# Expert layers that take four experts at a time in every step, with the first weight places given back in halves, and the decay gates of all heads of the gated linear attention made at once

## The reference

```python
def gla_mixer(x, w_in, gate_w, gate_b, norm_g, w_out):
    z = x @ w_in
    q, k, v, r, glr = jnp.split(z, [...], axis=-1)
    loga = log_sigmoid(einsum('bsgr,grk->bsgk', glr, gate_w) + gate_b) / 16     # decay gates, 4 heads, 2 directions
    o = gla_chunked(q, k, v, loga_forward) + flipped(gla_chunked(... loga_backward))
    return (silu(r) * head_norm(o, norm_g)) @ w_out

def ec_moe(x, w_router, w_gate, w_up, w_down):                                  # 16 experts, 32 tokens each
    aff = softmax(einsum('bnd,de->bne', x, w_router))
    gates, idx = top_k(swapaxes(aff, 1, 2), 32)
    xin = x[bidx, idx]
    h = silu(einsum('becd,edf->becf', xin, w_gate)) * einsum('becd,edf->becf', xin, w_up)
    out = einsum('becf,efd->becd', h, w_down) * gates[..., None]
    return zeros_like(x).at[bidx, idx].add(out)

for i in range(2):
    h = (mlstm_mixer if i == 0 else gla_mixer)(x, ...)
    x = layer_norm(ALPHA * x + h, ...)
    x = layer_norm(ALPHA * x + ec_moe(x, ...), ...)
```

## Time and profile before

| | |
|---|---|
| median of the runs | 2774.12 us (2769.06 to 2780.21) |
| the profiled execution | 2774.46 us, span of its instructions 2772.7 us |
| mean granted TensorE clock | 0.962 |
| busy: PE, DVE, ACT, POOL | 2492.2, 1249.6, 955.9, 77.7 us |
| moved by DMA | 692.63 MB, 250 GB/s over the span |
| matmuls of L1849 | 453.3 us gate and up, 203.9 us down |
| PE idle before L1849, ended by DMA | mostly `weight_ring<-in_moe_w_gate`, 50.4 us |

### The profile page before, as it was taken

One profiled execution on the slowest core, in us unless ns is written; L12 is line 12 of the kernel. 1 busy time (PEld: TensorE's weight loads), 2 busy tenths in 40 slices (PEclk: granted clock), 3 DMA queues, 4 the chain that ended last, 5 costly groups with the idle time before them and its releaser, 6 DMA issues.

```text
span 2772.7 us, 32444 instructions
## 1 busy us (share of the span) xinstructions
PE 2492.2 (90%) x13553; PEld 1716.4 (62%) x13553; DVE 1249.6 (45%) x1906; ACT 955.9 (34%) x1526; POOL 77.7 (3%) x79
## 2 busy tenths in 40 slices
PE   9899788877999798878987989999999999988998
PEld 7642222226742233227875877888888888887887
DVE  6521000017622000007565564675567567576774
ACT  5420000007521000004445344554365465444653
POOL 0001000001001000001000000000200000011000
PEclk9999999998999999998998999999999999999999
DMA  7489999994499999999323434555545555544451
GB/s 277 168 332 404 423 428 428 428 395 167 158 381 413 426 426 426 428 386 254 119 77 99 155 125 169 158 191 193 174 144 189 190 182 193 165 157 148 153 196 70
DMA packets 231234, 692.63 MB, mean 250 GB/s; under 512 B 36497, under 2 KB 136801, under 8 KB 207152
## 3 DMA queue, kind: packets, MB, share of 16 engines
q1 hardware_dynamic: 229296, 686.24, 66.5%
q0 software_dynamic: 1792, 4.31, 0.6%
HBM read 687.10 MB, written 5.28 MB: 250 GB/s over the span
## 4 chain that ended last, share of the span: by engine, by line
PE 64%; DMA 16%; DVE 11%; ACT 5%; issue 2%; SPq 1%; PEld 0%; POOL 0%; DVEq 0%; POOLq 0%; ACTq 0%; PEldq 0%
PE accumulators L563 25%; PE accumulators L1849 14%; PE accumulators L3449 12%; DMA weight_ring<-in_moe_w_gate 7%; DMA weight_ring<-in_moe_w_up 7%; PE accumulators L3450 6%; DVE weight_lows L287 3%; DMA weight_ring<-in_moe_w_down 2%; ACT weight_highs L278 1%; PE accumulators L1725 1%; ACT arena L2765 1%; SPq L440 1%; DVE arena L2785 1%; PE accumulators L323 0%; PE accumulators L1775 0%
## 5 line engine op out<-in xcount | busy, mean ns | idle before, releaser
L287 DVE TENSOR_TENSOR weight_lows<-weight_ring,weight_highs 128x1024 fp32r<-128x1024 f32 (+1 forms) x504 | 608.2, 1232 | 394.5 <-ACT weight_highs L278 389.8
L278 ACT CAST weight_highs<-weight_ring 128x1024 fp32r<-128x1024 f32 (+1 forms) x504 | 513.6, 1043 | 280.2 <-PE accumulators L563 260.5
L1849 PE MATMUL accumulators<-weight_ring,arena 128*32 128x512 f32 x1952 | 453.3, 615 | 93.2 <-DMA weight_ring<-in_moe_w_gate 50.4
L3449 PE MATMUL accumulators<-xT_halves,weight_highs 128*128 128x512 f32 x1408 | 492.8, 396 | 1.3 <-DVE xT_halves L847 1.3
L3450 PE MATMUL accumulators<-xT_halves,weight_lows 128*128 128x256 f32 x1408 | 392.0, 278 | 0.0
L1849 PEld LDWEIGHTS accumulators<-weight_ring,arena 128*32 128x32 f32 x1952 | 128.1, 113 | 408.4 <-issue 408.2
L563 PE MATMUL accumulators<-weight_highs,arena_halves 128*128 128x512 f32 x1040 | 332.1, 396 | 7.1 <-issue 3.9
L563 PE MATMUL accumulators<-xT_halves,weight_highs 128*128 128x256 f32 (+2 forms) x1584 | 306.6, 295 | 12.8 <-DVE xT_halves L1066 5.0
L3449 PEld LDWEIGHTS accumulators<-xT_halves,weight_highs 128*128 128x128 f32 x1408 | 264.8, 188 | 64.4 <-issue 2.0
L563 PEld LDWEIGHTS accumulators<-xT_halves,weight_highs 128*128 128x128 f32 (+2 forms) x1584 | 256.3, 199 | 20.8 <-issue 12.6
L3450 PEld LDWEIGHTS accumulators<-xT_halves,weight_lows 128*128 128x128 f32 x1408 | 265.3, 188 | 0.0
(11 more groups left out here) (456 smaller groups left out, 2177.8 us busy)
## 6 DMA issues: line engine op xcount, KB each, us to landing
weight_ring<-in_moe_w_up SPq DMA_DIRECT2D x64, 2048.0 KB, 17.3
weight_ring<-in_moe_w_gate SPq DMA_DIRECT2D x58, 2048.0 KB, 17.7
weight_ring<-in_moe_w_down SPq DMA_DIRECT2D x56, 2048.0 KB, 17.3
weight_ring<-in_ffn_w_gate SPq DMA_DIRECT2D x44, 1024.0 KB, 5.3
weight_ring<-in_ffn_w_up SPq DMA_DIRECT2D x44, 1024.0 KB, 5.3
weight_ring<-in_ffn_w_down SPq DMA_DIRECT2D x44, 1024.0 KB, 4.9
weight_ring<-in_l_w_in SPq DMA_DIRECT2D x38, 1024.0 KB, 5.1
weight_ring<-in_moe_w_down SPq DMA_DIRECT2D x32, 512.0 KB, 14.8
```

The lines of the kernel that those rows point to most:

```text
L278: act.copy(p.high(), p.raw()).then_inc(self.high_ready, 1)
L287: dve.tensor_tensor(p.low(), p.raw(), p.high().bitcast(F32), ALU.subtract).then_inc(self.low_ready, 1)
L1849: last = pe.matmul(acc[e * CAP:(e + 1) * CAP, half * BANK:(half + 1) * BANK], tokens, stream.part(first + e, c)[:, half * BANK:(half + 1) ...
L3449: pe.matmul(acc, high, m.xT_r[:, c, :, :].rearrange("p k t -> p (k t)"), start=(c == 0), stop=False, skip_group_check=True)
```

## The change

Four edits.

1. In every step TensorE takes all four experts: at j % 4 == 0 it waits for all four units and runs each chunk and half for e = 0 to 3; at other j it does only what else is hung there. So all four units of a step are given back at its end.
2. The first four units of each expert stream (`SPLIT`) are given back in halves, after chunk 1 and after chunk 3. Units below 13 (`SPLITS`) whose first slot comes free before the second are loaded as two halves of 1 MB; the loads of a stream are then sorted by the count they wait for.
3. The extra units are 6, 7 and 8 in place of 5, 6 and 7. `gather_second` moves from j == 2 to behind chunk 1 of the first step, amid its matmuls.
4. In gla the gates and sizes of all four heads come behind quarter (1, 0), with the exponentials; the logarithms move from (1, 2) to (1, 1), the sums one or two quarters earlier, and the first half of the decays by one quarter.

The diff, cut:

```diff
-EXTRA = (5, 6, 7)
-EXTRA_HOMES = ((("arena", 1024, 4),), (("arena", 5120, 4),), (("xT", 0, 2), ("arena", 11264, 2)))
+EXTRA = (6, 7, 8)
+SPLIT, SPLITS = 4, 13
+EXTRA_HOMES = ((("arena", 1024, 4),), (("xT", 0, 2), ("arena", 11264, 2)), (("arena", 5120, 4),))
...
     def add_pair(self, stream, u):
...
+        after = [free(k) for k in (slot, slot + 1)]
+        if after[0] < after[1] and u < SPLITS:
+            self.units += [(stream, u, after[k], k) for k in range(2)]
+            self.loads[slot] += 32
+        else:
+            self.units.append((stream, u, max(after), None))
+            self.loads[slot] += 16
+        first, end = stream.ends(u)
+        self.use_count = max(self.use_count, end)
...
+    def ends(self, u):
+
+        if u < SPLIT:
+            return self.begin + u + 1, self.begin + SPLIT + u + 1
+        return self.begin + SPLIT + u + 1, self.begin + SPLIT + u + 1
...
-    return Stream(m, units + ends, (), len(units), EXTRA)
+    stream = Stream(m, units + ends, (), len(units), EXTRA)
+    start = next(i for i, x in enumerate(m.units) if x[0] is stream)
+    m.units[start:] = sorted(m.units[start:], key=lambda x: x[2])
+    return stream
...
-                        if j == 2:
-                            gather_second()
...
-                    duo = (0, 1) if j % 4 == 0 else (2, 3)
-                    for e in duo:
+                    if j % 4:
+                        continue
+                    for e in range(EQ):
                         stream.wait_loaded(pe, first + e)
...
                         for half in range(2):
-                            for e in duo:
+                            for e in range(EQ):
...
-                                if c == 3 and half == 1:
+                                if half == 1 and (c == 3 or (c == 1 and first + e < SPLIT)):
                                     last.then_inc(m.used, 1)
+                        if (q, j, c) == (0, 0, 1):
+                            gather_second()
...
-    DECAYS = ((1, 3), (2, 1), (2, 3), (3, 2))
-    EXPS = ((2, 0), (2, 1), (2, 2), (2, 3), (4, 0), (4, 1), (4, 2), (4, 3))
+    DECAYS = ((1, 2), (2, 0), (2, 2), (3, 1))
+    EXPS = ((1, 3), (2, 0), (2, 1), (2, 2), (4, 0), (4, 1), (4, 2), (4, 3))
...
                 if at == (1, 0):
-                    gates(0)
-                    gates(1)
-                if at == (1, 1):
-                    gates(2)
-                    gates(3)
+                    for h in range(H):
+                        gates(h)
...
                 if at == (1, 0):
                     act.wait_ge(s["bias_ready"], 1)
-                    sizes(0)
-                    sizes(1)
-                if at == (1, 1):
-                    sizes(2)
-                    sizes(3)
+                    for h in range(H):
+                        sizes(h)
                     for h in range(H):
                         exponential(h)
-                if at == (1, 2):
+                if at == (1, 1):
                     for h in range(H):
                         logarithm(h)
```

## The result

The change makes the kernel slower: 2843.54 us median of 4 runs (2839.07 to 2850.88) against 2773.71 us for the kernel before (2769.06 to 2780.21), a ratio of 1.0245 (95% interval 1.0222 to 1.0268). The forecast was 2773 us, range 2751 to 2787; the kernel is 70 us above it and outside the range, on the side to which 0.16 was given. The profiled execution took 2839.07 us, its span is 2837.3 us (2772.7 before).

What follows compares the result with a forecast made beforehand. Arrival of weights was taken to bound the expert stages, ring places their first quarter. From 2774.5 us: less 17.2 early gain, plus 21.0 for holes, less 5 in gla, gives 2773.3, forecast as 2773 us; range 2751 to 2787.

Steps and rivals of the forecast that it cites:

- What bounds the kernel: Expert stages: arrival of weights sets all but the first quarter, places in the ring set that quarter.
- The early gain: First quarter of both expert stages: places come back sooner, 11.0 and 6.2 us gained, together 17.2 us.
- the second hole: First expert stage: DMA's standstill from 194 to 198 us, claimed to go.
- The price of an instruction: Steps of four experts: 0.1075 us for each matmul instruction, so 6.9 us for 64.
- Halves: Start of both expert stages: sixteen 1 MB loads overlap when queued and cost 0 to 1.7 us.
- Rival 4: Start of both expert stages: halves do not overlap and cost 46 us, 2819 us in all; chance 0.01.
- The cold step: Weight-bound steps of four: start at the low clock after long waits and take 9.2 us.
- The hole: Weight-bound steps of four: DMA stands still for 9.2 + 1.1 - 9.8 = 0.5 us, 0.7 with the thin queue.
- The number of steps that pay: From the fourth step of four on: 19 in the first expert stage, 11 in the second, 21.0 us lost.
- gla: Gla stage: gates of all heads at once bring head 0's products earlier, 5 us gained, bounds 1 and 8.
- rival 2: Steps of four from the fourth on: low clock lasts longer, step 9.9 us, 2796 us in all; chance 0.14.
- the last sentence: Expert stages: the forecast would be wrong altogether if the queue held more than two units at a landing.

Runs made afterwards that it cites:

- e1: The changed kernel with four experts at once only in the first three steps of each expert stage, then two at a time; 2757.46 us, ratio 0.9922.
- e10: As e1, but six steps of four experts per expert stage (the whole first quarter of the experts) instead of three; 2774.58 us, ratio 0.999.
- e7: The changed kernel with two experts in all steps; halves for the first four units, moved gather, extras and gla edit stay; 2771.66 us, ratio 0.9982.
- e5: The kernel before with the edit of the gla stage alone, expert layers untouched; 2773.86 us, ratio 0.9985.
- e8: The changed kernel with half the products (chunks 0 and 3) in every step of four but the first; 2771.54 us, ratio 0.9973.
- e11: The changed kernel with three quarters of the products (chunks 0, 1, 3) in every step of four but the first; 2797.44 us, ratio 1.0065.
- e6: The changed kernel with every unit given back and loaded in halves, from unit 13 on ordered two units at a time; 2776.22 us, ratio 0.9993.
- e3: The changed kernel with unread matmuls filling PE's waits in the first expert stage from its second quarter on; 2825.69 us in one run.

## Why the prediction was wrong

**What bounds the kernel, and the first quarter: right.** The early gain was forecast at 11.0 and 6.2 us; e1 has 10.8 and 7.1, in stages that scatter by 3 us and more. Flow restarts at 162.7 us, 4.6 behind PE's start (forecast 4.4), and 191 to 200 us runs at 422 GB/s, so the second hole is gone. The price of an instruction (forecast 0.1075, measured 3.64 us for 32, 0.114 with the tail of the last) and of a full step (6.9, measured 7.07 in e10) held. e7 adds what the text said only in passing: it is PE's halved work that makes the gain possible. The halves alone bring 4.4 and 0.9 us in the profile, and e7, which has the gla edit too, is only 2.2 us faster than e5 by the medians.

**Halves: right in substance.** 1 MB loads overlap; they flow at 419 GB/s where the ring is fed all the time. By these rates 16 of them cost under 1 us (forecast 0 to 1.7). Rival 4 is refuted.

**The cold step: right.** Forecast 9.2 us; the mean of 14 steps is 9.2. A stretch of the step that starts at 336.71 (the clock column is the third last, 1.2 GHz at 0.50) is at the low clock for 4.7 us, much as the earlier trace rows:
```profile
336.80:341.50 4.70, 4.70 (x24) 1.23 (x28) 0.00 (x0) 0.00 (x0) 0.00 (x0) 0.50 0.99 425
```
The Trainium skill's rule ("TensorE: Matmul & The Clock Gate", HAM oscillation — how this bites in real kernels) holds here: the 15 steps from 294.09 to 598.22 us take 8.6 to 10.1 us, none the 7.07 of full speed. By the table of e8 and e11 the low clock is about half of the price; the prediction made it the whole (0 at full speed).

**The hole: this step failed.** The prediction wrote: "When the fourth unit of a group lands, only two units, 9.8 us of DMA, are queued behind it", and made the hole step + 1.1 - 9.8 = 0.5 us. When PE sees the landing, part of that reserve has already been moved. From issue to landing the second load of a burst takes 11.6 to 12.1 us in 12 of the 14 turns and 13.2 and 13.6 in the others. The two loads are 9.8 us of transfer, and the flow starts some 1.0 us behind the issue, so about 1.2 us are left over, in which DMA goes on at its full rate. The bytes say the same. From the end of a step to the next landing, in an ordinary turn and in the latest:

```profile
346.70:358.86 12.16, 1.16 (x8) 0.97 (x8) 2.44 (x2) 0.00 (x0) 0.00 (x0) 0.74 0.95 384
518.31:532.20 13.89, 0.00 (x0) 0.00 (x0) 0.69 (x1) 0.59 (x1) 0.00 (x0) 0.68 0.95 388
```
These are 4.67 and 5.39 MB, where the two awaited loads hold 4.19. So 0.5 MB of the reserve is gone at the ordinary landing and 1.2 MB at the late one: 8.7 us are left of it, or 7.0, not 9.8. With the step of 9.2 that makes the hole some 1.6 us and more. Whether the awaited bytes had all moved by then and only their landing came late, or bytes of later loads had gone ahead of them, these views don't tell apart. The change in stretches of one us, behind the step of 336.71 and that of 294.09:

```profile
345.00:346.00 1.00, 1.00 (x16) 0.27 (x8) 0.00 (x0) 0.00 (x0) 0.00 (x0) 1.00 0.09 33
346.00:347.00 1.00, 0.59 (x8) 0.00 (x0) 0.27 (x1) 0.00 (x0) 0.00 (x0) 1.00 0.00 0
```
```profile
301.00:302.00 1.00, 1.00 (x12) 0.27 (x8) 0.00 (x0) 0.00 (x0) 0.00 (x0) 1.00 0.08 33
302.00:303.00 1.00, 1.00 (x12) 0.14 (x4) 0.00 (x0) 0.00 (x0) 0.00 (x0) 1.00 0.08 33
```
The reserve ended 8.3 us behind the start of the one step and 6.9 us behind that of the other, whose turn also had two layer norm loads of 512 KB in its queue. The mean turn of 21.7 us against 19.6 gives 2.1 us a step; 0.7 was forecast. The row for this was there: a 1 MB load that lands alone takes 5.3 us, and 2.45 of it is transfer. I used it only to price halves. The Trainium skill has such a term too ("DMA: Bandwidth & Descriptors", 🔬 Anatomy of one DMA — SWDGE (gpsimd) path): for what GpSimd issues, a transfer costs about 2.0 us beside its bytes at 436 GB/s, most of it the receipt behind the last byte. These loads are issued by SyncE. If the figure is carried over, two loads of 2.1 MB take 2.0 + 9.6 = 11.6 us, an estimate from that page; this trace has 11.6 to 12.1 us.

**The number of steps that pay: failed too.** 19 and 11 were forecast, since a memory piece of 512 KB was to cover eight steps of stage 1. A stage has 20 steps from the fourth on, not 19. Stage 1 lost 40.4 us over its 20, 2.0 each, nearly what stage 0 lost. The pieces cover part of the hole only: the four turns from 974.76 to 1063.65 us, with a piece each, take 22.1 to 22.3 us, where their bytes need 19.6 + 1.2 = 20.8. 40 x 2.2 = 87 us in place of 30 x 0.7 = 21: these two terms make 66 us, and the profiles differ by 64.6 where the sum of the forecast was -1.2. Of it, the size of the hole alone makes 30 x 1.5 = 45 us, the ten further steps 22.

**gla: right.** Forecast 5 us; e5 has 4.2, interval 0.6 to 7.8. PE's wait for head 0 falls to 6.0 us in the change and in e1 too. The stage takes 163.2 to 166.1 us in the twelve kernels with the edit and 167.4 and 169.2 in the two without. That the change's profile shows 1.4 us, e1's 2.6 and e5's 4.2 is within that scatter.

**The rivals.** The side was that of rival 2, its mechanism wasn't: it asked for a step of 9.9 us, and the step kept to 9.2. What would have found it was said in the last sentence, with the wrong sign: I looked for a queue that holds more than two units at a landing, and it held less. The ranges for the cold step were carried through with care, while the 9.8 had no range at all.

**Sum.** Against the profile of before: -2.8 (start, scatter), stage 0 -10.8 + 46.5, gla -1.4, stage 1 -7.1 + 40.4, rest -0.2 = +64.6 us.

## What to carry to other kernels

When places of a ring are given back in a group, follow the loop round once before you build it: step, release, issue, time from issue to landing of the last load that the next step needs. If its sum is above the transfer time of the group, every turn pays the difference, and the time from issue to landing is to be read from a row, not from bytes over rate. Take the larger step only where the engine is the bound, and go back to the smaller one where loads are; within a large step, give the first places back early, and keep the pieces of one unit together in the queue.

## What the runs showed of the hardware

- The engine that waits sees a load land later than its bytes over the rate: 11.6 to 12.1 us from issue to landing for two loads of 2 MB from an empty queue, of which 9.8 are transfer and 1.0 the start. DMA moves some 0.5 MB of the loads behind them before that landing.
- Landings are not evenly late. In the change two of 14 come 1.3 and 1.7 us later than the rest (13.2 and 13.6 for 11.9), with DMA near its full rate meanwhile. The flow behind a landing can end in a tail of 16 to 33 GB/s for 1 to 2 us, about one sixteenth of the full rate. That would fit one of the 16 DMA engines being behind the others; it wasn't tried, and the cause is open.
- Loads of 1 MB (8 KB for each partition) flow at 419 GB/s (e6) where those of 2 MB flow at 427 (e1), both with DMA busy throughout.
- Raising the clock over most of the time didn't shorten all steps behind a wait: 8.77 us in e3 behind waits of 2.5 and 2.6 us, but 7.07, the full speed, behind waits of 3.0 and 3.9 us. What decides between the two was not found.
